# Expert 31's weights in 4 KB runs, the sample rows as quarters, and a reordered final stage

## What is computed

```python
for e in range(N_EXPERTS):
    a = t @ p['w_gate'][e]
    u = t @ p['w_up'][e]
    out = out + combine[:, e:e + 1] * ((jax.nn.silu(a) * u) @ p['w_down'][e])
x = x + out                      # residual
y = x * rsqrt(mean(x * x) + EPS) * final_norm_g
```

## Time and profile before

| what | us |
|---|---|
| median of 3 executions | 736.8 (736.21 to 737.12) |
| the profiled execution | 734.72 |
| its span, first to last instruction or transfer | 733.0 |
| TensorE busy | 652.5 (89%) |
| VectorE busy | 251.0 (34%) |
| mean granted TensorE clock | 0.982 of full speed |

### The profile page before, as it was taken

One profiled execution on the slowest core, in us unless ns is written; L12 is line 12 of the kernel. 1 busy time (PEld: TensorE's weight loads), 2 busy tenths in 40 slices (PEclk: granted clock), 3 DMA queues, 4 the chain that ended last, 5 costly groups with the idle time before them and its releaser, 6 DMA issues.

```text
span 733.0 us, 9145 instructions
## 1 busy us (share of the span) xinstructions
PE 652.5 (89%) x3164; PEld 314.2 (43%) x3164; DVE 251.0 (34%) x516; ACT 161.5 (22%) x317; POOL 95.4 (13%) x161
## 2 busy tenths in 40 slices
PE   8999999999998899996899999877878776778995
PEld 4478888874455533332233333322222222223331
DVE  7798997187266520101010111100000100001057
ACT  3677511232432111110011111101000101001033
POOL 5100000000000212122012122211211112111000
PEclk9999999999999899997899999999999999999998
DMA  9533005469736899999999999999999999999983
GB/s 326 218 115 114 3 1 203 170 256 430 284 118 258 323 412 425 426 421 421 429 426 424 425 425 421 424 423 427 424 424 426 427 424 425 427 424 423 417 344 121
DMA packets 30004, 246.52 MB, mean 336 GB/s; under 512 B 6064, under 2 KB 6576, under 8 KB 16896
## 3 DMA queue, kind: packets, MB, share of 16 engines
q1 hardware_dynamic: 23216, 233.95, 77.1%
q0 software_dynamic: 5280, 8.21, 3.1%
q10 hardware_dynamic: 1456, 3.62, 1.3%
HBM read 235.65 MB, written 19.20 MB: 348 GB/s over the span
## 4 chain that ended last, share of the span: by engine, by line
PE 48%; DMA 36%; DVE 10%; ACT 3%; issue 2%; SPq 0%; POOLq 0%; POOL 0%; DVEq 0%
PE psA L1407 25%; DMA mem<-in_w_gu 25%; PE psB L1407 21%; DMA mem<-in_w_down 7%; DVE mem L731 4%; DMA mem<-hn_d,mem 2%; DVE mem L955 1%; DMA mem<-in_w_vb 1%; ACT front_c L665 1%; DMA hn_d<-front_c 1%; DVE mem L870 1%; ACT mem L673 1%; DVE mem L882 1%; PE psA L1412 1%; DVE mem L912 1%
## 5 line engine op out<-in xcount | busy, mean ns | idle before, releaser
L1407 PE MATMUL psA<-mem 128*64 128x512 f32 (+8 forms) x1368 | 309.0, 515 | 26.5 <-DMA mem<-in_w_gu 16.4
L1407 PE MATMUL psB<-mem 128*64 128x512 f32 (+7 forms) x1210 | 267.1, 540 | 31.6 <-DMA mem<-in_w_gu 20.3
L1407 PEld LDWEIGHTS psA<-mem 128*64 128x64 f32 (+4 forms) x1368 | 142.3, 151 | 174.4 <-issue 126.3
L1407 PEld LDWEIGHTS psB<-mem 128*64 128x64 f32 (+3 forms) x1210 | 109.0, 152 | 172.5 <-issue 123.0
L731 DVE TENSOR_TENSOR mem<-mem 128x512 f32<-128x512 f32 (+17 forms) x116 | 67.6, 597 | 23.7 <-ACT mem L565 19.6
L1163 DVE TENSOR_TENSOR front_c<-front_c,psA 64x512 f32<-64x512 f32 x15 | 10.3, 690 | 175.8 <-ACT front_c L665 175.8
L1163 DVE TENSOR_TENSOR front_c<-front_c,psB 64x512 f32<-64x512 f32 x15 | 10.3, 690 | 171.3 <-ACT front_c L665 171.3
L1325 POOL DMA_INDIRECT y_d<-front_c,mem x30 | 30.8, 1028 | 268.3 <-ACT front_c L676 268.3
L1320 POOL DMA_INDIRECT mem<-hn_d,mem x34 | 36.0, 1058 | 94.6 <-DMA hn_d<-front_c 65.4
L665 ACT ACTIVATE front_c<-psA 64x512 f32<-64x512 f32 x15 | 8.8, 589 | 121.6 <-PE psA L1407 121.6
L665 ACT ACTIVATE front_c<-psB 64x512 f32<-64x512 f32 x15 | 8.8, 589 | 115.3 <-PE psB L1407 115.3
(11 more groups left out here) (246 smaller groups left out, 365.3 us busy)
## 6 DMA issues: line engine op xcount, KB each, us to landing
mem<-in_w_gu SPq DMA_DIRECT2D x63, 2048.0 KB, 33.4
mem<-in_w_down SPq DMA_DIRECT2D x31, 2048.0 KB, 37.6
mem<-in_w_out SPq DMA_DIRECT2D x2, 2048.0 KB, 8.4
y_d<-mem SPq DMA_DIRECT2D x1, 4096.0 KB, 11.8
mem<-y_d SPq DMA_DIRECT2D x8, 512.0 KB, 8.4
mem<-in_x_T SPq DMA_DIRECT2D x8, 260.0 KB, 8.8
mem<-in_w_vb SPq DMA_DIRECT2D x8, 256.0 KB, 8.9
mem<-in_x_prompt SPq DMA_DIRECT2D x4, 512.0 KB, 11.2
```

The costliest lines, as they stand in the source:

```text
L1407: return nc.tensor.matmul(out, lhsT, rhs, start=start, stop=stop, skip_group_check=True)
```

## The change

- The three units of expert 31 (`FINE = 3`) come as four transfers each, of 512 KB, with runs of 4 KB in each partition in place of 16 KB; `place_of` counts accordingly.
- The sample's 8 rows of 1024 are laid out as quarters: quarter q of row r is on partition 32q + r, 256 columns wide. Their residual and the gain come in eight small loads, their y rows in two indirect gathers by GpSimd with row numbers written early (`quarter_rows`), and their result leaves by an indirect scatter. The sum of squares of the four quarters is joined by a small matrix product (`same_row`). The added buffers are cleared by GpSimd between the first two expert steps.
- On VectorE `add_rows(0)` stands ahead of expert 31's silu product; before, all additions stood behind it.
- The order becomes 0, sample, 1, 2, 3. Tile 3, the last, is summed in PSUM; tiles 0, 1, 2 and the sample get their kept part by `add_kept` on VectorE. Before, tiles 0 and 1 were summed in PSUM.

```diff
+            pieces = 4 if q >= 3 * NE - FINE else 1
-            return q % NSLOT, (q // NSLOT + 1 + before) * 16
+            return q % NSLOT, (q // NSLOT + pieces + before) * 16
...
+            def load_by_blocks(q):
+                e, j = UNITS[q]
+                s = q % NSLOT
+                for k in range(4):
+                    block = slice(2 * DE * k, 2 * DE * k + 2 * DE)
+                    unit(s, (ring[:, s, block], (w_dn[e] if j == 2 else w_gu[2 * e + j])[:, block]))
...
             sp.dma_start(gfb, a["final_norm_g"].unsqueeze(0).to_broadcast([128, D])).then_inc(rest_in, 16)
+            sp.wait_ge(tokens_rdy, 2)
+            for q in range(4):
+                at = slice(32 * q, 32 * q + NS)
+                sp.dma_start(gfq[at], a["final_norm_g"][WQ * q:WQ * q + WQ].unsqueeze(0).to_broadcast([NS, WQ])).then_inc(rest_in, 16)
+                sp.dma_start(xq[at], x2_d[NP_:NTOK, WQ * q:WQ * q + WQ]).then_inc(y_in[4], 16)
             sp.wait_ge(gu_ps, NE - 2)
             sp.wait_ge(dn_ps, NE - 2)
...
-            for t in LAST_ORDER:
-                add_rows(t)
+            add_rows(0)
+            dve.wait_ge(sg_rdy, NE)
+            V.tensor_tensor(hh[0:64, 1, :], sg[64:128, 1, :], psB[64:128, 1, :], ALU.mult).then_inc(h_done, 1)
+            for t in (1, 2, 3):
+                add_rows(t)
+            dve.wait_ge(picks_rdy, 2)
+            add_rows(4)
...
+            add_kept(0, 1)
+            add_kept(4, 2)
+            add_kept(1, 3)
+            dve.wait_ge(rest_in, 16 * 9)
+            scaled(0, 1)
+            add_kept(2, 4)
+            scaled(1, 2)
+            scaled(2, 3)
+            dve.wait_ge(f_rt, 4)
+            link(V.reciprocal(scaleq, rootq))
+            V.scalar_tensor_tensor(xq, xq, scaleq, gfq, ALU.mult, ALU.mult).then_inc(f_done, 1)
+            scaled(3, 5)
...
+            pool.wait_ge(consts, 5)
+            for c in range(3):
+                for q in range(4):
+                    link(G.iota(quarter_rows[32 * q:32 * q + 32, c:c + 1], [[0, 1]], base=4 * (c * NTOK + NP_ if c < 2 else 0) + q, channel_multiplier=4))
...
+            for c in range(2):
+                G.indirect_dma_start(out=(yq0, yq1)[c], out_offset=None, in_=y2_d.rearrange("t (q n) -> (t q) n", q=4),
+                                     in_offset=bass.IndirectOffsetOnAxis(ap=quarter_rows[:, c:c + 1], axis=0),
+                                     bounds_check=8 * NTOK - 1, oob_is_err=False).then_inc(xg_in[c], 16)
+            pool.wait_ge(f_done, 4)
+            G.indirect_dma_start(out=o[1].rearrange("b l (q n) -> (b l q) n", q=4),
+                                 out_offset=bass.IndirectOffsetOnAxis(ap=quarter_rows[:, 2:3], axis=0),
+                                 in_=xq, in_offset=None, bounds_check=4 * NS - 1, oob_is_err=False).then_inc(y_out[0], 16)
...
+            pe.wait_ge(tokens_rdy, 2)
+            pe.wait_ge(picks_rdy, 2)
+            kept(0)
+            for q in range(4):
+                ins = mm(LAST_PS[4][32 * q:32 * q + 32], picks[:, NP_:NP_ + 32], y_kept[:, WQ * q:WQ * q + WQ], True, True)
+            ins.then_inc(f_ps, 1)
+            kept(1)
+            kept(2)
+            pe.wait_ge(f_acc, 4)
+            pe.wait_ge(f_sum, 1)
+            for h in range(2):
+                mm(LAST_PS[3][:, h, :], ident[:, :], x2[:, 3, 512 * h:512 * h + 512], True, False)
+            pe.wait_ge(f_sq, 2)
+            for q in range(4):
+                ins = mm(ROW_SUMS[32 * q:32 * q + 32], same_row, sumq, True, True)
+            ins.then_inc(f_ps, 1)
+            kept(3)
```

More of the change, by code:

```diff
@@ L213, in build @@
         ylast = y_kept[64:128]
-        picks = view(20480, NTOK)
+        picks = view(20480, NP_ + 32)
         tokens = cut(1024, NTOK)[64:128]
@@ L218, in build @@
         tok_cw = tiny[64:128, 92:96]
+        WQ = D // 4
+        xq, yq0, yq1, gfq = (view(16384 + WQ * k, WQ) for k in range(4))
+        cwq, sumq, rootq, scaleq = tiny[:, 20:22], tiny[:, 22:23], tiny[:, 23:24], tiny[:, 24:25]
+        same_row = st[:, 0:32]
+        quarter_rows = sb("quarter_rows", [128, 3], i32)
         psA = ctx.enter_context(nc.psum_tensor("psA", [128, 4, 512], f32))
@@ L420, in _ @@
                     sp.wait_ge(dn_ps, e_old + 1)
-                load(q)
+                if q < 3 * NE - FINE:
+                    load(q)
+                else:
+                    load_by_blocks(q)
             sp.dma_start(gfb, a["final_norm_g"].unsqueeze(0).to_broadcast([128, D])).then_inc(rest_in, 16)
+            sp.wait_ge(tokens_rdy, 2)
[3 more added lines that the diff above has]
+                sp.dma_start(xq[at], x2_d[NP_:NTOK, WQ * q:WQ * q + WQ]).then_inc(y_in[4], 16)
             sp.wait_ge(gu_ps, NE - 2)
@@ L427, in residual @@
                 sp.dma_start(x2[0:ROWS[t], t, :], x2_d[t * 128:t * 128 + ROWS[t], :]).then_inc(y_in[t], 16)
-            for t in LAST_ORDER[0:3]:
+            for t in range(2):
                 residual(t)
@@ L433, in _ @@
                 sp.wait_ge(y_out[u], 16 * (NE // 2 - 1))
-            for n, t in enumerate(LAST_ORDER):
-                if n >= 3:
+            for t in range(4):
+                if t >= 2:
                     residual(t)
@@ L439, in _ @@
                     sp.dma_start(yin[0:ROWS[t], 2 * t + c, :], y2_d[r0:r0 + ROWS[t], :]).then_inc(y_in[t], 16)
[L440 to L444, removed]
+            for t in range(4):
+                sp.wait_ge(f_done, t + 1 if t < 3 else NT)
+                sp.dma_start(o[0][0, t * 128:(t + 1) * 128, :], x2[:, t, :]).then_inc(f_out, 16)
+            sp.wait_ge(f_out, 16 * 4)
+            sp.wait_ge(y_out[0], 16 * (NE // 2))
         @block.scalar
@@ L704, in _, with root_of_sum @@
                 A(ylast[:, 512 * h:512 * h + 512], psB[64 * h:64 * h + 64, 3, :], ACT.Copy).then_inc(y_last, 1)
[L706 to L716, removed]
+            def root_of_sum(t, total):
+                A(halves(yin[:, 2 * t, :]), total, ACT.Square, accum_out=fx[:, t:t + 1]).then_inc(f_sq, 1)
+                act.wait_ge(f_sq, t + 1 if t == 0 else t + 2)
+                A(ss[:, 2, t:t + 1], fx[:, t:t + 1], ACT.Sqrt, scale=1.0 / D, bias=epsc[:, :]).then_inc(f_rt, 1)
+            act.wait_ge(f_sum, 1)
+            root_of_sum(0, halves(x2[:, 0, :]))
+            act.wait_ge(f_sum, 2)
+            A(yq0, xq, ACT.Square, accum_out=sumq).then_inc(f_sq, 1)
+            for t in (1, 2):
+                act.wait_ge(f_sum, t + 2)
+                root_of_sum(t, halves(x2[:, t, :]))
+            act.wait_ge(f_ps, 5)
+            A(rootq, ROW_SUMS, ACT.Sqrt, scale=1.0 / D, bias=epsc[:, :]).then_inc(f_rt, 1)
+            act.wait_ge(f_ps, 6)
+            root_of_sum(3, LAST_PS[3])
         @block.vector
@@ L1195, in picks_of @@
             def picks_of(k):
-                return V.tensor_scalar(picks[64 * k:64 * k + 64], tokens, tok_cw[:, k:k + 1], tok_cw[:, 2 + k:3 + k], ALU.is_equal, ALU.mult)
+                return V.tensor_scalar(picks[64 * k:64 * k + 64, 0:NTOK], tokens, tok_cw[:, k:k + 1], tok_cw[:, 2 + k:3 + k], ALU.is_equal, ALU.mult)
             picks_of(0)
             picks_of(1).then_inc(picks_rdy, 1)
+            dve.wait_ge(tokens_rdy, 2)
+            V.tensor_reduce(same_row, ident[:, :].rearrange("p (q r) -> p r q", q=4), AX.X, ALU.add)
+            for q in range(4):
+                ins = V.tensor_copy(cwq[32 * q:32 * q + NS], cw[0:NS, :, 4])
+            ins.then_inc(picks_rdy, 1)
             tile_step(1, 1)
@@ L1214, in _ @@
             further(x1, x2_, psB, psA)
-            dve.wait_ge(sg_rdy, NE)
-            V.tensor_tensor(hh[0:64, 1, :], sg[64:128, 1, :], psB[64:128, 1, :], ALU.mult).then_inc(h_done, 1)
             def add_rows(t):
-                r = ROWS[t]
-                dve.wait_ge(y_in[t], 48)
+                dve.wait_ge(y_in[t], 48 if t < 4 else 64)
+                if t == 4:
+                    dve.wait_ge(xg_in[0], 16 * (NE // 2 + 1))
+                    dve.wait_ge(xg_in[1], 16 * (NE // 2 + 1))
+                acc, rows, by = ((x2[:, t, :], yin[:, 2 * t:2 * t + 2, :], cw[:, :, t]) if t < 4
+                                 else (xq, view(16384 + WQ, 2, WQ), cwq))
                 for j in range(2):
-                    ins = V.scalar_tensor_tensor(x2[0:r, t, :], yin[0:r, 2 * t + j, :], cw[0:r, j, t:t + 1], x2[0:r, t, :],
-                                                 ALU.mult, ALU.add)
+                    ins = V.scalar_tensor_tensor(acc, rows[:, j], by[:, j:j + 1], acc, ALU.mult, ALU.add)
                     if j == 0:
@@ L1238, in scaled @@
[L1238 to L1254, removed]
+            dve.wait_ge(picks_rdy, 2)
+            add_rows(4)
+            def add_kept(t, count):
+                dve.wait_ge(f_ps, count)
+                dve.wait_ge(f_acc, t + 1)
+                total = halves(x2[:, t, :]) if t < 4 else xq
+                tt(total, total, LAST_PS[t], ALU.add).then_inc(f_sum, 1)
@@ L1386, in _ @@
             tile_step(0, 0, 0, before=False)
```

(19 more changed lines are left out.)

18 lines of the change are left out of this document (10 added, 8 removed).

## The result

| | before | after |
|---|---|---|
| median | 736.55 us (4 runs, 736.21 to 737.12) | 740.97 us (4 runs, 738.84 to 742.26) |
| profiled execution | 734.72 us | 738.84 us |
| its span | 733.0 us | 737.1 us |

The ratio is 1.0053 with a 95% interval of 1.0029 to 1.0076: by the medians the changed kernel is 4.4 us slower. That lies 0.8 us above the upper end of the range, 740.2 us, and the forecast was 737.9 us, the same within 0.2%.

The account below looks back on a forecast made before the run. The end was taken as set by when y rows land and VectorE's work behind them. Rows land later, that work stays 13.8 us, the store 3.0 us: 736.8 + 1.1 = 737.9 us, range 733.6 to 740.2.

Parts of the forecast that it names:

- Late rows: Final stage: tile 0's y rows land at 706.95 us in place of 705.62, the last y rows at 717.3 for 716.2.
- TensorE's gap: Ahead of expert 31's transposes: TensorE is 3.1 us late, as tile 0's additions now precede the silu product.
- The late product is hidden: TensorE's first kept product ends near 718.0 us, but VectorE asks for it later, so TensorE's delay costs nothing.
- VectorE's end: VectorE ends at 731.1 us against 729.98, with 13.8 us of work behind the last landing, as before.
- SyncE's last wait: End of the program: the span ends 1.1 us later, at 734.1 us, with the last store behind VectorE's end.
- The quarters and the two new kept sums: VectorE, final stage: quarters save 3.3 us; two new kept sums cost 2.4 us, one dropped saves 1.2; waits take the rest.
- The store behind it takes 3.0 us as before.: End of the program: from VectorE's last product to the end of the span, 3.0 us, unchanged.
- rival D: The sample's store by GpSimd ends between 1.4 us before the last store and 3.3 us after; chance 0.13 with C.
- C: Expert 31's 4 KB pieces move at a slower rate, rows land 2.3 us later, time 740.2 us; chance 0.13 with D.
- The 4 KB runs: Expert 31's units as twelve transfers: 0.6 us on the DMA engines, bounds 0 and 2.9 us.
- one queue that never runs dry: The late-finishing DMA engines stay busy from 700.5 to 716.2 us, so releasing the y loads earlier moves nothing.
- B: With 4 KB runs the scatter lands some 3 us sooner and the y loads follow; time 733.8 us; chance 0.29.

Follow-up runs that it names:

- run 4: The changed kernel with expert 31's silu product moved back ahead of tile 0's additions; ratio to the kernel before 1.0054.
- run 7: The changed kernel with the sample stored from ScalarE's queue, expert 31's product ahead of the additions and its units as single transfers; ratio to before 0.9997.
- run 1: The changed kernel with the sample stored by four plain transfers from ScalarE's queue, not by GpSimd's indirect scatter; ratio to before 1.0014.
- run 2: The kernel before, with GpSimd waiting at the end for VectorE's last scaling and then clearing one column, no DMA; ratio 1.0036.
- runs 6 and 10: The kernel before with two more 512 KB loads queued just ahead of the residual tiles, the same kernel timed twice; ratios 1.0011 and 1.0025.
- run 9: The kernel before with GpSimd clearing 2048 unused columns between its last scatter's landing and the release of the y loads; ratio 1.0022.
- run 8: run 7 with tile 3's additions moved behind the sample's additions and the kept sums of tile 0 and the sample; ratio to before 0.9979.
- 12: run 8 with tile 2 summed in PSUM like tile 3; ratio to the kernel before 0.9969.
- 13: 12 with expert 31's units in 4 KB runs again (FINE = 3); ratio to the kernel before 0.9974.

## Why the prediction was wrong

**What held.** Late rows: rows 0 were put at 706.95 and tile 3's at 717.3; less the 0.36 us by which this execution was early they are 706.6 and 716.9, measured 706.53 and 716.68. TensorE's gap: 3.1 us, measured 3.13. The late product is hidden: run 4. VectorE's end: 731.1 less 0.36 is 730.7, measured 730.69; that it fits so closely is partly luck, as the last rows came 0.2 us sooner than forecast and the work behind them took 14.0 us in place of 13.8. SyncE's last wait: the span was to end 1.1 us later without a new wait at the end, and SyncE was done 1.0 us later (733.8 against 732.8). The quarters and the two new kept sums about cancel: run 7 is at 0.9997.

**The step that failed.** "The store behind it takes 3.0 us as before." That held for the store and not for the program. I had named the mechanism's place, rival D, the sample's store from GpSimd, but priced it by the landing of the scatter alone (3.1 to 8 us from its issue) and took "before". The landing was as I took it: 3.4 us, at 733.56. What I didn't price is that the engine has an end of its own. Its DRAIN took 5.6 us in the trace of the kernel before, from 698.9, and I had looked at what engines do and not at how they close. The end of GpSimd's last instruction moved from 699.0 to 731.2, and 731.2 + 5.7 = 736.9, 3.1 us past SyncE's end at 733.8. SyncE itself was done 1.0 us later than before (1.07 us of VectorE less the 0.36, and 0.3 us more from there to SyncE's end), and 3.1 + 1.0 is the 4.1 us between the two spans. Runs 1 and 2 show it from both sides.

The range had a fault of its own: its upper end was C's 740.2 us, while D's own bound, a scatter that ends 3.3 us after the last store, gives 737.9 + 3.3 = 741.2 us. The measured 740.97 us lies inside that, but by another mechanism: not the scatter but the engine's closing came last.

The Trainium skill, VectorE: DVE Perf Modes, section The DRAIN you can't avoid, says that the DRAINs of the preamble and postamble are some 12 ns on all five engines. SyncE's 7 ns is of that order. The rows of VectorE (1324 ns, from 728.7) and ScalarE (324 ns, from 728.2) in the kernel before begin with the engine's last operation (728.70 + 1.28, 728.17 + 0.29) and end within 0.1 us of it, as TensorE's (3958 ns, from 720.3) does of its last product (722.29 + 1.88). Only GpSimd's lasts: it ends 5.5 us behind its clearing, so there the measurement decides.

**Terms that were off or unsettled.** The 4 KB runs: charged 0.6 us, and the two pairs of runs give +1.0 and -0.5 us on rows 0, with ratios of 1.0001 alone and 1.0067 against 1.0053; not told from zero. That the rows landed as late as forecast is therefore not explained term by term. The reason given for late rows, one queue that never runs dry and doesn't wait for the release, was half right: extra loads are paid in full (runs 6 and 10), but a release that was 2.8 us later was paid for too, and the queue ran dry (run 9). An earlier release by more than a few tenths was never reached, so B isn't disproved as an effect of an early release; its first step fell, since 4 KB runs made the scatter's wait 6.73 us where it had been 6.96, not 3 us shorter. The Trainium skill, DMA: Bandwidth & Descriptors, section Queues, rings and completion order, lets an engine round-robin between queues by the packet. If a packet grew with the run, smaller runs should have let the scatter through much sooner, and the traces don't show that. What makes the scatter wait 7 us is open. The half clock behind TensorE's gap was not in the forecast; the first kept product ended at 718.9 and not near 718.0, still before VectorE took it at 720.23. It cost nothing in the changed kernel's profile and 0.70 us in run 1's, where VectorE was left waiting for a kept product.

## What to carry to other kernels

Before you give an engine the last instruction of a program, look at how it closes: list the DRAIN of each engine, and count from the end of its last instruction to the end of the DRAIN as part of the path. Keep GpSimd's last work, even a one-column clearing, well ahead of the end, and store from a queue whose engine closes fast. Where a final stage waits for a load in the middle of its additions, reorder so that work that needs no load stands there; in run 8 that gave 0.9979, where narrower operations alone (run 7) gave 0.9997.

## What the runs showed of the hardware that I had not expected

- GpSimd's closing DRAIN takes 5.6 us when its last instruction is a small clearing, with the last DMA landed (before and run 2), and 5.7 us from the end of an indirect scatter's issue (changed kernel), which is 3.3 us behind the scatter's landing. Behind two gathers, just issued, it ran to about 8 us past their issue (run 7: the second was issued until 703.5, the DRAIN ended at 711.5). In the five runs that end on the gathers (1, 7, 8, 12, 13) it ended 2.8 to 2.9 us behind the landing of the second gather, while the time from its issue ranged from 7.9 to 8.6 us; so the landing seems to set the end there, though no run tests it.
- SyncE took much longer to issue while many transfers were outstanding, against 0.33 us for a plain issue. What the limit is, a count or bytes, is not shown. In the changed kernel its first eight pieces took 34.1 us to issue and the last four 9.6 us, and it was free at 690.3, in time for the release:

```profile
641.72 34.10 SPq L343 DMA_DIRECT2D mem<-in_w_gu  x8
675.86 9.64 SPq L343 DMA_DIRECT2D mem<-in_w_down  x4
```

- Behind a gap of 3.13 us that ended at 709.91 TensorE's granted clock went to 0.50 from 711 to 714 us. In the kernel before a gap of 2.70 us that ended at 622.77 was followed by 16 matmuls in 3.65 us, the time they take at full clock, while in run 9 a gap of 2.75 us that ended at 680.58 was followed by a clock of 0.50 until 683 us and 5.00 us for the same matmuls.
